# Output projections of a two-layer encoder step: units of 512 moving columns, each in two steps over half of the rows

## What is computed

```python
# layer 0: o is the attention's result
hp = hp + o @ w_o                                  # "out0": 1152x1024 by 1024x1024
hp = hp + sq_relu_mlp(rmsnorm(hp, norm_ffn[0]), w_up, w_down)
# layer 1
o = rmsnorm(o, norm_g).reshape(B, T, GLA_HEADS * GLA_DV) * silu(g)
hp = hp + o @ w_o                                  # "out1": 1152x1024 by 1024x1024
hp = hp + sq_relu_mlp(rmsnorm(hp, norm_ffn[1]), w_up, w_down)
```

## Time and profile before

| | |
|---|---|
| median of 3 runs | 2862.81 us (2862.7 to 2865.65) |
| span of the profiled execution | 2858.9 us, 3.9 us under the median |
| TensorE busy | 2763.3 us, 97% of the span |
| VectorE, ScalarE, GpSimd busy | 2010.4, 1307.0, 396.3 us (70%, 46%, 14%) |
| `out0` | 643 to 777 us of the span |
| `out1` | 2011 to 2128 us of the span |

### The profile page before, as it was taken

The page is one execution under the profiler, slowest core; times in us unless marked ns, Lnnn a source line. Parts: engine busy times, 40 slices in busy tenths (PEclk is TensorE's granted clock), DMA queues, the critical chain, the costliest instruction groups (busy, mean ns, idle before and its releaser), DMA issues. The chain is left out here.

```text
span 2858.9 us, 47631 instructions
## 1 busy us (share of the span) xinstructions
PE 2763.3 (97%) x17783; PEld 2501.0 (87%) x17783; DVE 2010.4 (70%) x3144; ACT 1307.0 (46%) x2177; POOL 396.3 (14%) x421
## 2 busy tenths in 40 slices
PE   8999999989999999999999999998999999999998
PEld 8889877659989988999889899987998998889987
DVE  4389889953597788877882266537268778887787
ACT  3377568782334444544441144434133543445433
POOL 2222111112100000000012154437210000000000
PEclk9999999999999999999999999999999999999999
DMA  4412621325132322323204333248423233132331
GB/s 152 111 56 86 156 67 23 62 74 167 62 112 72 100 90 64 108 71 100 93 30 151 111 102 97 84 146 284 130 69 98 72 100 98 64 100 71 100 101 74
DMA packets 220750, 279.30 MB, mean 98 GB/s; under 512 B 30434, under 2 KB 174754, under 8 KB 220595
## 3 DMA queue, kind: packets, MB, share of 16 engines
q1 hardware_dynamic: 220450, 276.68, 30.9%
q10 hardware_dynamic: 144, 0.52, 0.0%
HBM read 220.13 MB, written 57.03 MB: 97 GB/s over the span
## 5 line engine op out<-in xcount | busy, mean ns | idle before, releaser
L1353 DVE TENSOR_TENSOR h<-mlp_dn_acc,h 128x512 f32<-128x512 f32 x308 | 200.8, 684 | 20.1 <-PE mlp_dn_acc L1204 19.1
L464 PE MATMUL acc<-mid_w_hi,mid_xT_hi 128*128 128x256 f32 x648 | 190.3, 294 | 6.6 <-PEq L572 3.8
L464 PE MATMUL acc<-mid_w_lo,mid_xT_hi 128*128 128x256 f32 x648 | 184.9, 285 | 0.0
L464 PE MATMUL acc<-mid_w_hi,mid_xT_lo 128*128 128x256 f32 x648 | 184.9, 285 | 0.0
L1204 PE MATMUL mlp_dn_acc<-end_w_hi 128*128 128x512 f32 x392 | 155.2, 396 | 3.5 <-DVE end_w_lo L1326 3.0
L1204 PE MATMUL mlp_dn_acc<-end_w_hi,early 128*128 128x512 f32 x400 | 157.8, 395 | 0.0
L1204 PE MATMUL mlp_dn_acc<-end_w_lo,end_w_hi 128*128 128x512 f32 x392 | 155.0, 396 | 0.0
L464 PEld LDWEIGHTS acc<-mid_w_hi,mid_xT_hi 128*128 128x128 f32 x648 | 125.9, 194 | 7.6 <-issue 4.5
L2630 ACT ACTIVATE att_logits<-att_logits,att_neg_max 128x528 f32<-128x528 f32 (+8 forms) x144 | 111.3, 773 | 32.7 <-DVE att_neg_max L2694 32.2
L464 PEld LDWEIGHTS acc<-mid_w_hi,mid_xT_lo 128*128 128x128 f32 x648 | 126.0, 194 | 0.0
L464 PEld LDWEIGHTS acc<-mid_w_lo,mid_xT_hi 128*128 128x128 f32 x648 | 125.7, 194 | 0.0
(11 more groups left out here) (575 smaller groups left out, 9573.8 us busy)
## 6 DMA issues: line engine op xcount, KB each, us to landing
mlp_pool_w<-x_sums SPq DMA_DIRECT2D x84, 576.0 KB, 3.7
mlp_pool_w<-in_ffn_w_up SPq DMA_DIRECT2D x42, 512.0 KB, 4.8
spare_w<-in_ffn_w_down SPq DMA_DIRECT2D x32, 512.0 KB, 3.9
proj_w_raw<-in_a_w_in SPq DMA_DIRECT2D x8, 1024.0 KB, 5.9
mid_w_raw<-in_ffn_w_down SPq DMA_DIRECT2D x16, 512.0 KB, 4.3
end_w_raw<-in_ffn_w_down SPq DMA_DIRECT2D x16, 512.0 KB, 4.2
x_sums<-mlp_pool_w SPq DMA_DIRECT2D x24, 288.0 KB, 2.2
spare_w<-in_b_w_in SPq DMA_DIRECT2D x6, 1024.0 KB, 5.6
```

Source lines behind the costliest of these rows:

```text
L464: mm = pe.matmul(self.acc[:, i % NA, 0:u["n"]], x[c][:, k, u["t"] * P:(u["t"] + 1) * P], w[a][:, s, k, 0:u["n"]], start=(n == 0), stop=(n ...
L1353: dve.tensor_tensor(dst, acc, dst, ALU.add).then_inc(added, 1)
```

## The change

Both projections move from `gemm_phase` to a new `out_phase` with the class `Wide`.

- A chunk has 512 columns, so there are two chunks ("columns" 0 and 1) and 18 units. A unit is computed in two steps, r = 0 over weight rows 0 to 511 and r = 1 over rows 512 to 1023, each of 4 blocks x 3 terms = 12 matmuls of 128x512. A piece of weights is 512 rows by 512 columns, 1 MB as before, in the same two slots, viewed as four blocks (`wide_of`).
- Steps run in groups: r = 0 of three units, then r = 1 of the same three, the sum staying in their banks; `out1` begins with a group of four and one of two, since `state` has done r = 0 of two units.
- DVE makes all low halves but `out1`'s first, each as one subtraction of 128x2048. POOL keeps only the norm's small operations.
- DVE adds the residual in 18 operations of 128x512 instead of 36 of 128x256; the residual's DMAs are half as many and twice as large.
- In `state`, SP loads both pieces of the first column (2 MB instead of 1 MB), and ACT waits for both before it makes the first's high half. `raw1` is allocated before `state` instead of after it; the order of the `end_` tensors stays.
- The instructions of the last column's norm stay, in the new order of steps.

```diff
+class Wide(Gemm):
+    KH = KB // 2
+    def steps(self, g, runs=(3, 3, 3)):
+        us, out = list(self.of[g]), []
+        for n in runs:
+            now, us = us[:n], us[n:]
+            out += [(0, u) for u in now] + [(1, u) for u in now]
+        return out
+    def act_w_hi(self, act, hi):
...
+        if hi >= 2 and hi % 2 == 0:
+            act.wait_ge(self.first_done, hi // 2)
+        elif hi >= 2:
+            act.wait_ge(self.unit_done, self.of[hi // 2 - 1][-1]["i"] + 1)
+        act.activation(self.whole(self.sh.whi, hi), self.whole(self.sh.raw, hi), ACT.Copy).then_inc(self.whi_done, 1)
+    def make_w_lo(self, e, hi, parts=1):
...
+    def pe_step(self, pe, r, u):
+        i, NA, g = u["i"], self.NA, u["c"]
+        hi = 2 * g + r
+        if u is self.of[g][0] and hi > 0:
+            pe.wait_ge(self.wlo_done, hi)
+        if r == 0 and i >= NA:
+            pe.wait_ge(self.unit_out, i - NA + 1)
...
+        for k in range(self.KH):
...
+            for a, c in TERMS:
+                mm = pe.matmul(self.acc[:, i % NA, 0:u["n"]], x[c][:, self.KH * r + k, u["t"] * P:(u["t"] + 1) * P],
+                               w[a][:, k, :], start=(r == 0 and n == 0), stop=(r == 1 and n == last))
...
+        steps = [gm.steps(0, (3, 3, 3) if st else (4, 2, 3))] + [gm.steps(g) for g in range(1, G)]
...
+            def _(act):
...
+                for t in range(NT):
+                    if t == NT - GRP:
+                        gm.act_w_hi(act, gm.halves)
+                    tail.act_sumsq(act, t)
+                    if t >= 2:
+                        tail.act_hi(act, t - 2)
...
+            def _(pe):
...
+                for g in range(G):
+                    for r, u in steps[g]:
+                        if r == 0 and u["i"] < begun:
+                            continue
+                        if st and g == 0 and r == 0:
+                            if u["i"] + 1 < NT:
+                                st.pe_transpose(pe, u["i"] + 1)
+                            st.wait_ready(pe, u["i"] + 1)
+                        gm.pe_step(pe, r, u)
+                        if g == G - 1 and r == 1 and u["t"] >= 2:
+                            tail.pe_transpose(pe, u["t"] - 2)
...
+            def _(dve):
...
+                for g in range(G):
+                    for r, u in steps[g]:
...
+                        if r == 0 and u is gm.of[g][-1]:
+                            gm.make_w_lo(dve, 2 * g + 2)
+                        if r == 1:
+                            gm.dve_evacuate(dve, u)
+                            if g == G - 1 and u["t"] >= 1:
+                                tail.dve_norm(dve, u["t"] - 1)
+                            if g == G - 1 and u["t"] >= 2:
+                                tail.dve_lo(dve, u["t"] - 2)
+                            if g < G - 1 and u is gm.of[g][-1]:
+                                gm.make_w_lo(dve, 2 * g + 3)
...
-                sp.dma_start(sh.raw0[:, :, :], next_w.rearrange("(k p) n -> p k n", p=P)).then_inc(next_in, 16)
+                for raw, half in zip((sh.raw0, sh.raw1), next_w):
+                    sp.dma_start(wide_of(raw[:, :, :]), half.rearrange("(k p) n -> p k n", p=P)).then_inc(next_in, 16)
...
-                        act.wait_ge(next_in, 16)
+                        act.wait_ge(next_in, 32)
```

More of the change, by code:

```diff
@@ L325, in __init__ @@
         if residual is not None:
-            self.res = b.sb("residual", [P, NB, CW])
+            self.cw = chunks[0]["w"].shape[1]
+            self.res = b.sb("residual", [P, NB, self.cw])
         self.units = units = []
@@ L419, in sp_load_res @@
                 sp.wait_ge(self.unit_out, u["i"] - self.NB + 1)
[L420 to L421 removed]
+            c0 = u["c"] * self.cw
+            sp.dma_start(self.res[:, u["i"] % self.NB, :], self.residual(u["t"])[:, c0:c0 + self.cw])\
                 .then_inc(self.res_in[u["i"] % self.NB], 16)
@@ L3234, in next_unit @@
                     n = 0
-                    for k in range(KB):
+                    for k in range(KB // 2):
                         for a, c in TERMS:
-                            mm = pe.matmul(dS[:, 2 * t:2 * t + 1, :], (sh.xhi, sh.xlo)[c][:, k, t * P:(t + 1) * P],
-                                           (sh.hi0, sh.lo0)[a][:, k, :], start=(n == 0), stop=(n == len(TERMS) * KB - 1))
+                            mm = pe.matmul(next_acc[:, t, :], (sh.xhi, sh.xlo)[c][:, k, t * P:(t + 1) * P],
+                                           wide_of((sh.hi0, sh.lo0)[a][:, :, :])[:, k, :], start=(n == 0), stop=False)
                             n += 1
@@ L3461, in encoder @@
                 h = inner.enter_context(nc.sbuf_tensor("h0", [P, NT, D], F32))
-                gemm_phase(nc, "out0", sh, [chunk(a_w_o[0], c, CW, "N", "resid", None) for c in range(0, D, CW)],
-                           src_dram=tile_of(o), residual=either(xp, xs), h=h, next_w=ffn_w_up[0][:, 0:CW],
-                           next_gamma=norm_ffn[0], loaded=True, order=ATT_ORDER,
-                           there=[spare_x[:, i * D:(i + 1) * D] for i in range(2)], banks=ring, follow="T",
-                           last_stored=(o_last, 16 * (KVH // 2 * 2 * (HEADS // KVH) + 4)))
+                out_phase(nc, "out0", sh, [chunk(a_w_o[0], c, D // 2, "N", "resid", None) for c in range(0, D, D // 2)],
+                          either(xp, xs), h, ffn_w_up[0][:, 0:CW], norm_ffn[0], src_dram=tile_of(o), loaded=True, order=ATT_ORDER,
+                          there=[spare_x[:, i * D:(i + 1) * D] for i in range(2)], banks=ring,
+                          last_stored=(o_last, 16 * (KVH // 2 * 2 * (HEADS // KVH) + 4)))
                 spare_2.close()
@@ L3489, in encoder @@
         h = ctx.enter_context(nc.sbuf_tensor("h1", [P, NT, D], F32))
-        gemm_phase(nc, "out1", sh, [chunk(b_w_o[0], c, CW, "N", "resid", None) for c in range(0, D, CW)],
-                   preset=True, pre=2, residual=tile_of(hd), h=h, next_w=ffn_w_up[1][:, 0:CW], next_gamma=norm_ffn[1],
-                   banks=[acc_e[:, 0, :], acc_e[:, 1, :], None, None], follow="T")
+        out_phase(nc, "out1", sh, [chunk(b_w_o[0], c, D // 2, "N", "resid", None) for c in range(0, D, D // 2)],
+                  tile_of(hd), h, ffn_w_up[1][:, 0:CW], norm_ffn[1], banks=[acc_e[:, 0, :], acc_e[:, 1, :], None, None], begun=2)
         mlp_phase(nc, "mlp1", sh, h, ffn_w_up[1], ffn_w_down[1], norm_final, x_sums, y=either(yp, ys), banks=[acc_e[:, 0, :], acc_e[:, 1, :], None, None, None, None],
```

157 lines of the change are left out of this document (148 added, 9 removed).

## The result

The changed kernel takes 2846.3 us (median of 4 runs, 2844.5 to 2847.9), the kernel before beside it 2862.8 (4 runs, 2859.7 to 2865.7). A repeat gave 0.9951 (0.9938 to 0.9965).

The account below looks back on a forecast made before the run. The prediction took TensorE's distance between matmul starts as the bound in both projections. Its terms, -7.6 + 0.1 + 0.3 = -7.2 us, took the median from 2862.8 to 2855.6 us, range 2852 to 2859.5 us, chance 0.70.

Parts of the forecast that it names:

- What bounds the kernel: Whole kernel: TensorE, busy 97% of the span; inside both projections the distance between matmul starts sets the time.
- Part 1: Matmuls of `out0` and `out1`: 432 of 512 columns instead of 864 of 256; -5.1 and -2.5 us, sum -7.6 us.
- rival A: Matmuls: the surplus grows with the columns, so two of 256 are worth one of 512; 2861.2 us, chance 0.18.
- the fixed 2.5 ns: Matmuls: a skill page's fixed cost per warm matmul; halving their number would give only 2.2 us, time 2861.0 us.
- Part 2: Transposes and first column of both projections: transposes cancel, second weight pieces arrive in time, so nothing waits.
- 0.9 us to spare: First column of `out0`: margin by which the second weight piece is ready before its first r = 1 step.
- Part 3: Last column's waits: -1.9 us at tile 0, +1.2 at tile 5 in `out1`, +0.8 at tile 8 in `out0`; +0.1 us.
- Rival B: Last column: VectorE sets the pace, 4.05 us a tile against TensorE's 3.65; about 2866 us, chance 0.12.
- Part 4: `state`: ScalarE waits for a second megabyte of weights, 0 to 3 us late; +0.3 us, bounds 0 and 2.
- The MLPs keep their tensors' places and their code: nothing: MLPs: unchanged places and code, so no change in time.
- the last paragraph: Signs in the changed trace; a change in the phases behind, held to be the same, would make the forecast wrong.

## Why the prediction was wrong, point by point

- **What bounds the kernel:** right. TensorE's busy share is 97% before and after, and spacing and waits of TensorE explain the phases.
- **Part 1, the matmuls:** right in kind and nearly in size. `out0`: 0.228 us forecast, 0.2275 measured. `out1`: 0.232 forecast, 0.2296 measured, worth 432 x 0.0024 = 1.0 us, and this is the term that was mis-sized in the projections: I had taken it from `mlp1`, where the `end_` tensors stand behind other work, and the row of `mlp0` was as near. The surplus over the columns' own time (0.2133 us) is 14 to 16 ns at 512 columns against 11 to 13 at 256, so rival A, the doubled surplus, is out, and so is the fixed 2.5 ns that the Trainium skill ("TensorE: Matmul & The Clock Gate", "Wait — 56ns, not 53.3ns?") gives.
- **Part 2, the first column:** right, no wait for the second piece in either phase. The "0.9 us to spare" were thin: with GpSimd's 4.58 us in the place of VectorE's 2.29 a wait of 0.83 appears at just that point.
- **Part 3, the waits:** the two of tile 0 are gone, tile 5 in `out1` waits 1.09 us (1.2 forecast) with the cause that was named, tile 8 in `out0` 0.40 (0.8 forecast), tile 8 in `out1` keeps its 1.07. Rival B, waits at every tile, did not come.
- **Part 4, `state`:** no cost of the second megabyte shows. A wait of 1.23 us for VectorE's `state_S_in` stands at 1965.4 us after and not before, but also in the run with `out0` alone changed, whose `state` is the old one (1.23), and not in that with `out1` alone, whose `state` is the new one (0.20). 0.3 us was forecast, and the stretch of `state` differs by more between profiles of the same kernel (87.2 and 86.1 us before, 87.5 and 85.7 after).
- **The step that failed is the last sentence of Part 4**, "The MLPs keep their tensors' places and their code: nothing", with its like in the last paragraph, where I hold the phases behind to be the same. Same code is not the same timing. I had looked at the waits of TensorE in the two projections only; the waits of 2.52 and 1.35 us in `proj1b`, and the long issues ahead of them, stood in the trace of before. What the runs showed in its place: the phases between, put at nothing, gained 4.6 us in the first pair of profiles, all of it in `proj1b` (z 243.4 to 238.5), through 3.5 us less of waits for `proj1b_a` and 3.9 us less at the low clock.

The account in ratios: -7.2 us forecast, 1.3 more from the phases themselves (-8.7 in the traces), and some 6 from `proj1b` (z 244.6 on average before, 238.2 after: 3.9 us of waits and 2.3 of clock) make -15, where the ratio says -14.6 with 1.8 either way. That the time came out below the range is thus no error of the projections' sum, and it was luck of position that the change moved the packets out of the bursts and not into them. The range failed because it had no term for anything outside the edited phases.

## What to carry to other kernels

Where the same work runs with half the matmuls, price it by the distance between starts in a row of the target shape on the same tensors, and then read the waits of the whole trace, not those of the edited phase. A small load that the bounding engine waits for, queued behind large stores on one DMA queue, can be a loss that comes and goes with an edit that changes the number of instructions, here by some 3 to 6 us of 2860; with the load ahead of the stores, no profile had a wait for it. Count with such a wait the low clock that may follow it, here 1.5 to 3 us behind waits of 1.2 to 2.5. To find out whether a gain elsewhere is luck of position, add instructions that do nothing, once a fraction of a packet and once a whole one.

## What the hardware showed that I had not expected

- The instruction queues move packets of 16.4 KB (`q8`, TensorE's; 1.64 MB / 100) and 8 KB (`q14`; 0.45 MB / 56) and stand in the DMA view among the packets of the same 16 engines as the data. In the bursts of the kernel before, an issue on SyncE's queue beside such a packet took 0.98 to 2.14 us instead of 0.45, and the 8 KB load landed after 3.9 us instead of 2.3 to 2.5. With a `q8` packet 1.5 to 2 us behind its issue (1769.9 and 1832.3 us before) it landed after 4.0 and 4.2 us, and TensorE did not wait for it. What inside the chip holds the issue back, no run shows.
- 96 instructions that compute nothing cost the changed kernel 3 us in a place some 1000 us later; 256 of them cost `proj1b` nothing.
- Behind waits of 2.52, 2.34, 1.18 and 1.33 us for `proj1b_a` the granted clock fell to 1.2 GHz for 3.4, 6.8, 3.4 and 3.4 us; behind waits of 1.35, 1.61 and 1.13 us it did not. What tells them apart, no run shows.
- 80 transposes of 8x8 took 2.15 us, 27 ns each with their loads.
- A subtraction of 128x2048 on GpSimd (4.60 us) held up VectorE's norm of 128x1024, with two inputs in SBUF, from 1.28 to 4.38 us, but not its addition with one input in PSUM (0.69 us).
